# The feed-forward norm of a second-block layer: rows split without the norm's root, the root applied to the results

## What is computed

```python
def rmsnorm(x, g):
    y = x * lax.rsqrt(jnp.mean(x * x, axis=-1, keepdims=True) + EPS)
    return y * g

for l in range(2):
    ...                                                   # three mixers, gated: y
    x = x + jnp.einsum('bsd,de->bse', y, w_out[l])        # output projection
    h = rmsnorm(x, norm_ffn_g[l])
    gu = jnp.einsum('bsd,df->bsf', h, w_ffn_in[l])        # 1024 -> 2 * 2816
    g_ff, u_ff = gu[..., :2816], gu[..., 2816:]
    g_ff = causal_dwconv(g_ff, ffn_conv_w[l], ffn_conv_b[l])   # 3 taps along the rows
    x = x + jnp.einsum('bsf,fd->bsd', silu(g_ff) * u_ff, w_ffn_out[l])
```

## Time and profile before

| | before |
|---|---|
| median of 3 runs | 2688.33 us (2687.64 to 2689.95) |
| the profiled execution | 2689.85 us, span from first to last instruction 2688.0 us |
| PE busy | 2414.5 us, 90% of the span |
| DVE, ACT, POOL busy | 1057.6, 745.9, 650.7 us (39%, 28%, 24%) |
| mean granted clock of TensorE | 0.934 of full speed |
| chain of work that ended last | PE 78%, DMA 7%, DVE 7%, issue 3%, ACT 3% |
| DMA engines | mean 112 GB/s |

### The profile page before, as it was taken

How to read it: one execution, slowest core, us unless ns; L and a number is a source line. 1 busy time by engine, 2 the same in 40 slices (tenths; PEclk the granted TensorE clock), 3 DMA queues, 4 the chain that set the end, 5 groups by cost and what they waited for, 6 DMA issues and landing times.

```text
span 2688.0 us, 31483 instructions
## 1 busy us (share of the span) xinstructions
PE 2414.5 (90%) x12390; PEld 1679.0 (62%) x12390; DVE 1057.6 (39%) x1863; ACT 745.9 (28%) x1176; POOL 650.7 (24%) x284
## 2 busy tenths in 40 slices
PE   7989688896777769989999999998988999999998
PEld 2334466544222248657876888887755887688886
DVE  2455455522011151565243656202165423466610
ACT  2333212211111113323222333212343222233311
POOL 0000000001000024213443444443320444344443
PEclk9999788876888879989998999999998999899999
DMA  4101700043999833212322333222210322233322
GB/s 187 47 24 39 144 3 2 2 178 138 406 411 408 327 110 110 64 32 71 96 93 70 95 100 97 79 99 81 91 55 23 95 94 94 70 95 95 101 80 85
DMA packets 80458, 301.86 MB, mean 112 GB/s; under 512 B 6944, under 2 KB 7328, under 8 KB 79808
## 3 DMA queue, kind: packets, MB, share of 16 engines
q1 hardware_dynamic: 72864, 277.97, 30.2%
q10 hardware_dynamic: 5152, 13.58, 1.3%
q0 software_dynamic: 2304, 8.39, 0.9%
HBM read 283.86 MB, written 24.97 MB: 115 GB/s over the span
## 4 chain that ended last, share of the span: by engine, by line
PE 78%; DMA 7%; DVE 7%; issue 3%; ACT 3%; POOL 0%; SPq 0%; DVEq 0%; ACTq 0%; another core or an unknown queue 0%; POOLq 0%
PE bank L1738 12%; PE bank L1740 12%; PE bank L1739 12%; DMA arena<-in_stream 5%; PE bank L527 5%; PE bank L1412 3%; PE bank L1876 3%; PE bank L1878 3%; PE bank L1877 3%; DVE arena L386 2%; PE bank L834 2%; PE bank L1725 2%; DVE arena L392 2%; PE bank L1723 2%; PE bank L1724 2%
## 5 line engine op out<-in xcount | busy, mean ns | idle before, releaser
L1483 POOL TENSOR_TENSOR ring_low<-ring,W_high 128x1024 fp32r<-128x1024 f32 x264 | 635.1, 2406 | 1080.5 <-ACT W_high L396 1080.5
L1738 PE MATMUL bank<-H_high,W_high 128*128 128x512 f32 x1408 | 562.8, 400 | 21.9 <-DVE H_low L386 11.3
L1739 PE MATMUL bank<-H_low,W_high 128*128 128x512 f32 x1408 | 554.5, 394 | 0.0
L1740 PE MATMUL bank<-H_high,ring_low 128*128 128x512 f32 x1408 | 554.1, 394 | 0.0
L396 ACT ACTIVATE W_high<-ring 128x1024 fp32r<-128x1024 f32 x264 | 279.7, 1060 | 974.7 <-PE bank L1740 603.9
L1738 PEld LDWEIGHTS bank<-H_high,W_high 128*128 128x128 f32 x1408 | 267.5, 190 | 102.8 <-issue 27.6
L1740 PEld LDWEIGHTS bank<-H_high,ring_low 128*128 128x128 f32 x1408 | 268.1, 190 | 57.1
L1739 PEld LDWEIGHTS bank<-H_low,W_high 128*128 128x128 f32 x1408 | 268.6, 191 | 55.1 <-issue 1.0
L396 ACT ACTIVATE arena<-bank 128x512 f32<-128x512 f32 (+4 forms) x275 | 130.3, 487 | 466.0 <-PE bank L809 120.2
L392 DVE SCALAR_TENSOR_TENSOR arena<-arena,bank 128x512 f32<-128x512 f32 (+2 forms) x116 | 55.5, 482 | 480.2 <-ACT arena L400 262.3
L1467 POOL DMA_INDIRECT sorted_x<-arena x8 | 7.9, 982 | 638.2 <-DVE arena L386 636.1
(11 more groups left out here) (222 smaller groups left out, 2955.0 us busy)
## 6 DMA issues: line engine op xcount, KB each, us to landing
ring<-in_stream SPq DMA_DIRECT2D x289, 512.0 KB, 3.6
arena<-in_stream SPq DMA_DIRECT2D x32, 2048.0 KB, 13.8
arena<-in_stream SPq DMA_DIRECT2D x32, 1024.0 KB, 10.6
sorted_x<-in_zero_row SPq DMA_DIRECT2D x1, 8704.0 KB, 49.0
arena<-sorted_x SPq DMA_DIRECT2D x17, 512.0 KB, 15.9
sorted_y<-arena ACTq DMA_DIRECT2D x16, 512.0 KB, 7.0
X<-in_x SPq DMA_DIRECT2D x1, 2048.0 KB, 9.0
out<-X ACTq DMA_DIRECT2D x8, 256.0 KB, 2.9
```

Source lines behind the costliest of these rows:

```text
L1483: G.tensor_tensor(ring_low[:, slot, :], ring[:, slot, :], W_high[:, s % 2, :].bitcast(F32), ALU.subtract).then_inc(po.tells("w_split"), 1)
L1738: mm(ps[:, :], wh[:, k, :], H_high[:, k, :], start=k == 0, stop=False)
L1739: mm(ps[:, :], wh[:, k, :], H_low[:, k, :], start=False, stop=False)
L1740: i = mm(ps[:, :], wl[:, k, :], H_high[:, k, :], start=False, stop=k == KD - 1)
```

## The change

The feed-forward products now run on `X * g_ffn` without the root. As each `wout` bank lands and DVE has added it to `X`, ACT writes the high part of `X * g` right away (`Identity` with the gains as scale, event `Lhh`) and then the squares, and DVE makes the low part in one instruction (event `Lh`) and adds the squares of the chunk to a running sum in `SQL[:, 0]` (event `Lsum` after the last). The sum over the features is one float32 product instead of eight, and stands in PE's order between `ffg0` and `ffu0`. The root goes to a buffer of its own (`ROOT`). DVE multiplies each `ffg` bank by `ROOT` on its way into `GP`, in place of ACT's copy, and there is one further DVE multiplication by `ROOT` for each `ffu`. The split of the slot of `ffu0` on ACT moves behind the last high part and the last square. The halved gate biases are written over themselves in `p2`, and the arena, a filling of the constants and an unused rest shrink to make room for `ROOT`. The transfers are the same but for 8 columns less of one load at the start.

```diff
@@ -201,9 +201,9 @@
     l += [f"gate{b_}_0" for b_ in range(3)]
     for m_ in range(8):
         l += [f"gate{b_}_{m_ + 1}" for b_ in range(3) if m_ < 7] + [f"br{b_}_{m_}" for b_ in range(3)]
-    l += [f"wout{m_}" for m_ in range(8)] + ["ssq4"]
+    l += [f"wout{m_}" for m_ in range(8)]
     for k in range(KF):
-        l += [f"ffg{k}", f"ffu{k}"]
+        l += [f"ffg{k}"] + (["ssq4"] if k == 0 else []) + [f"ffu{k}"]
     l += [f"fo{m_}" for m_ in range(8)]
     return {"A": a, "M": m, "B": [f"bias{h}" for h in range(DH)] + [f"gt{m_}" for m_ in range(8)], "L": l, "F": f}
 
...
@@ -270,12 +270,13 @@
             pass
         H_low = sb("H_low", [P, KD, T], F32R)
         W_high = sb("W_high", [P, 2, TPS * P], F32R)
-        sb("early_rest", [P, nCE + nA1 + nW1 - KD * T - 2 * TPS * P])
+        assert nCE + nA1 + nW1 == KD * T + 2 * TPS * P
         p1 = early[:, nCE:nCE + nA1]
         w1 = early[:, nCE + nA1:nCE + nA1 + nW1]
         cst = sb("cst", [P, nC])
         p2 = sb("p2", [P, nA2])
         small = sb("small", [P, 64])
+        ROOT = sb("root", [P, T])
         with nc.sbuf_tensor("arena", [P, ARENA], F32) as arena:
             pass
         arena_split = sb("arena_split", [P, ARENA], F32R)
...
@@ -1853,14 +1854,12 @@
                     pe.e.wait_ge(*pe.emptied(f"wout{m}"))
                     i = product(f"wout{m}", wh, wl, range(KD), Y_PARTS, ready="Ly" if m == 0 else None)
                     i.then_inc(pe.fills(f"wout{m}"), 1)
-                pe.e.wait_ge(*pe.emptied("ssq4"))
-                ps = bank_of("ssq4")
-                for c in range(KD):
-                    pe.e.wait_ge(*pe.nth("Lsq", KD + c + 1))
-                    i = mm(ps[:, :], cc("ones"), SQL[:, c, :], start=c == 0, stop=c == KD - 1)
-                i.then_inc(pe.fills("ssq4"), 1)
                 for k in range(KF):
                     chunk(f"ffg{k}", first=k == 0)
+                    if k == 0:
+                        pe.e.wait_ge(*pe.emptied("ssq4"))
+                        pe.e.wait_ge(*pe.nth("Lsum", 1))
+                        mm(bank_of("ssq4")[:, :], cc("ones"), SQL[:, 0, :], start=True, stop=True).then_inc(pe.fills("ssq4"), 1)
                     chunk(f"ffu{k}")
                 for m in range(8):
                     pe.e.wait_ge(*pe.emptied(f"fo{m}"))
...
@@ -1994,31 +1993,28 @@
                             sc.e.wait_ge(*sc.nth("Lbgate", 1))
                         if m >= 2:
                             sc.e.wait_ge(*sc.nth("Ly", m - 1))
-                        act_(TL[:, b + 3 * (m % 2), :], ps[:, :], ACT.Tanh, bias=arena_small("bgh", b * 8 + m), scale=0.5).then_inc(sc.takes(f"gate{b}_{m}"), 1)
+                        act_(TL[:, b + 3 * (m % 2), :], ps[:, :], ACT.Tanh, bias=q2("b_gate", b * 8 + m), scale=0.5).then_inc(sc.takes(f"gate{b}_{m}"), 1)
                     if m:
                         split_high(1)
                 split_high(1)
                 log_exp_tables()
                 for c in range(KD):
-                    split_high(1)
+                    if c < KD - 1:
+                        split_high(1)
                     sc.e.wait_ge(*sc.taken(f"wout{c}"))
+                    act_(H_high[:, c, :], X[:, c, :], ACT.Identity, scale=q2("g_ffn", c)).then_inc(sc.tells("Lhh"), 1)
                     act_(SQL[:, c, :], X[:, c, :], ACT.Square).then_inc(sc.tells("Lsq"), 1)
-                sc.e.wait_ge(*sc.filled("ssq4"))
-                ps = bank_of("ssq4")
-                log_of(sc, TL[:, 0, :], ps[:, :], EPS, 1.0 / D)
-                sc.e.wait_ge(sc.chain, sc.n)
-                inverse_root(TL[:, 0, :]).then_inc(sc.takes("ssq4"), 1)
+                split_high(1)
                 for k in range(KF):
                     split_high(1)
-                    sc.e.wait_ge(*sc.filled(f"ffg{k}"))
-                    ps = bank_of(f"ffg{k}")
                     if k == 0:
-                        sc.e.wait_ge(*sc.nth("Lh", 2 * KD))
-                        sc.e.wait_ge(*sc.nth("Lgpad", 1))
+                        sc.e.wait_ge(*sc.filled("ssq4"))
+                        log_of(sc, ROOT[:, :], bank_of("ssq4")[:, :], EPS, 1.0 / D)
+                        sc.e.wait_ge(sc.chain, sc.n)
+                        inverse_root(ROOT[:, :]).then_inc(sc.takes("ssq4"), 1)
+                    sc.e.wait_ge(*sc.taken(f"ffg{k}"))
                     if k >= 2:
                         sc.e.wait_ge(*sc.taken(f"ffu{k - 2}"))
-                    act_(GP[:, k % 2, 2:514], ps[:, :], ACT.Copy).then_inc(sc.takes(f"ffg{k}"), 1)
-                    sc.e.wait_ge(*sc.taken(f"ffg{k}"))
                     act_(TF[:, k % 2, :], GP[:, k % 2, 2:514], ACT.Identity, bias=q2("fcb", k), scale=q2("fcw", 2 * KF + k)).then_inc(sc.tells("Lfc"), 1)
                     split_high(1)
                     sc.e.wait_ge(*sc.nth("Lconv", k + 1))
...
@@ -2206,12 +2198,24 @@
                     dv.e.wait_ge(*dv.filled(f"wout{m}"))
                     ps = bank_of(f"wout{m}")
                     stt(X[:, m, :], ps[:, :], 0.5, X[:, m, :], ALU.mult, ALU.add).then_inc(dv.takes(f"wout{m}"), 1)
-                dv.e.wait_ge(*dv.taken("wout7"))
-                norm_split(dv, "ssq4", lambda c: q2("g_ffn", c))
+                    dv.e.wait_ge(*dv.nth("Lhh", m + 1))
+                    stt(H_low[:, m, :], X[:, m, :], q2("g_ffn", m), H_high[:, m, :].bitcast(F32), ALU.mult, ALU.subtract).then_inc(dv.tells("Lh"), 1)
+                    dv.e.wait_ge(*dv.nth("Lsq", KD + m + 1))
+                    if m:
+                        sq = tt(SQL[:, 0, :], SQL[:, 0, :], SQL[:, m, :], ALU.add)
+                        if m < KD - 1:
+                            st(sq)
+                        else:
+                            sq.then_inc(dv.tells("Lsum"), 1)
+                dv.e.wait_ge(*dv.taken("ssq4"))
                 V.memset(GP[:, :, 0:2], 0.0).then_inc(dv.tells("Lgpad"), 1)
                 for k in range(KF):
                     c = TF[:, k % 2, :]
                     g = GP[:, k % 2, :]
+                    dv.e.wait_ge(*dv.filled(f"ffg{k}"))
+                    if k == 0:
+                        dv.e.wait_ge(*dv.nth("Lgpad", 1))
+                    tt(g[:, 2:514], bank_of(f"ffg{k}")[:, :], ROOT[:, :], ALU.mult).then_inc(dv.takes(f"ffg{k}"), 1)
                     dv.e.wait_ge(*dv.nth("Lfc", k + 1))
                     st(stt(c, g[:, 1:513], q2("fcw", KF + k), c, ALU.mult, ALU.add))
                     stt(c, g[:, 0:512], q2("fcw", k), c, ALU.mult, ALU.add).then_inc(dv.tells("Lconv"), 1)
...
@@ -2219,6 +2223,7 @@
                     dv.e.wait_ge(*dv.nth("Lconv", k + 1))
                     t = TF[:, 5, :]
                     st(stt(t, TF[:, 2 + k % 2, :], 1.0, c, ALU.add, ALU.mult))
+                    st(tt(t, t, ROOT[:, :], ALU.mult))
                     dv.e.wait_ge(*dv.filled(f"ffu{k}"))
                     ps = bank_of(f"ffu{k}")
                     tt(t, t, ps[:, :], ALU.mult).then_inc(dv.takes(f"ffu{k}"), 1)
```

More of the change, by code:

```diff
@@ L54 @@
 R = 6
-ARENA = 55 * 512 + 40
+ARENA = 55 * 512 + 4
 TPS = 8
@@ L1627, in build @@
         BRANCH_PARTS = parts(chunks(*range(37, 45)), chunks(45, 46, 47, 48, 16, 17, 18, 19))
[L1629 removed]
+        TF0 = 512 * 37 + 1028 + 512 * 10
         TF = ch(TF0, 6)
[L1631 removed]
+        HIDDEN_PARTS = parts(chunks(*range(0, KF)), chunks(*range(26, 37)) + [512 * 37 + 1028 + 512 * i for i in range(10)] + [TF0 + 4 * 512])
         assert TF0 + 6 * 512 <= ARENA
[L1633 removed]
+        GP = arena[:, 512 * 37:512 * 37 + 1028].rearrange("p (n w) -> p n w", n=2)
         dunits = [(h, i) for h in range(DH) for i in range(NT)]
```

11 lines of the change are left out of this document (3 added, 8 removed).

## The result

| | before | changed |
|---|---|---|
| median | 2689.14 us (2687.64 to 2691.68, 4 runs) | 2640.60 us (2638.39 to 2641.12, 4 runs) |
| the profiled execution | 2689.85 us, span 2688.0 us | 2640.59 us, span 2638.8 us |
| PE busy | 2414.5 us | 2372.0 us |
| DVE, ACT, POOL busy | 1057.6, 745.9, 650.7 us | 1110.6, 734.5, 653.7 us |
| mean granted clock | 0.934 | 0.941 |

The ratio of the changed kernel to the one before is 0.9818, 95% interval 0.9803 to 0.9832. Faster was right, the size was not.

What follows compares the result with a forecast made beforehand. PE was taken to bound the kernel, with a stall and low clock at the norm before the feed-forward stretch. The median 2688.33 less 37.0 for two layers gave 2651.3 us, range 2648.5 to 2657.

Steps and rivals of the forecast that it cites:

- The stall: PE from `ssq4` to `ffu0`, at the norm: 24.91 and 24.93 us removed, 6.32 to 6.48 coming back in each layer.
- The sign: What would show it right, including no window at a clock below 1.00 between 1404 and 1830.
- the sum: Both layers' gain: 24.91 + 24.93 - 2 x (5.44 + 0.88) = 37.2 us; 37.0 was taken.
- The chain of `wout7`: Last bank to low part for `ffg0`, 2.6 us: ready about 1446.4, wanted at 1448.3, hidden with 1.9 us to spare.
- the thin cover: Split of `ffu0`, covered by the one `ssq4` product: in time by only 0.2 to 0.4 us.
- rival 1: At `ffu0`'s split or `wout7`'s chain, PE still waits 1 to 4 us a layer: 2653.5 to 2660 us; chance 0.10.
- rival 4: At `ffg0`, PE waits for the last rows as before; at three times the chain 3 us a layer, 2657; chance 0.02.
- The one product for eight: Between `ffg0` and `ffu0`, one `ssq4` product of 0.88 us comes back where eight took 7.03 us.
- The loop: Feed-forward loop, 22 times a layer: two added DVE multiplications by `ROOT`, 0.69 us each when free, cost PE nothing.
- rival 2: DVE's loop becomes the bound if `t` times `ROOT` is held: 11.77 us a k, 2690 us; chance 0.05 with similar losses.
- rival 3: In the loop, the multiplication into `GP` is held too: 13.5 us a k, 2766 us, slower; chance 0.03.
- The rest: Biases halved in place, smaller arena, 8 columns less in one load: same instructions on the same engines, worth nothing.

Runs made afterwards that it cites:

- Experiment 4: Changed kernel with the one sum product placed ahead of `ffg0` instead of between `ffg0` and `ffu0`: 2645.15 us, ratio 0.9836.
- experiment 8: Changed kernel without DVE's running sum, with eight products of the squares again between `ffg0` and `ffu0`: 2651.73 us, ratio 0.9861.
- experiment 1: Kernel before with only the new layout: smaller arena, unread `ROOT`, biases halved in place; arena at 116672: 2679.52 us, ratio 0.9966.
- experiment 2: Changed kernel with `p2` and `small` sharing 8 columns, so the arena starts 32 bytes earlier, at 116640: 2645.59 us, ratio 0.9836.
- experiment 11: Changed kernel with the arena right behind the constants and the padded banks `GP` moved to its end: 2632.91 us, ratio 0.9809.
- experiment 6: Changed kernel run once more, nothing altered: 2641.10 us, ratio 0.9818.
- experiment 12: Changed kernel with the arena behind the constants and `GP` at its end, timed again in five rounds: 2638.66 us, ratio 0.9818.

## Where the prediction was right, and where it failed

Forecast were 2651.3 us and a range of 2648.5 to 2657; measured were 2640.6. The mechanism of the main term came out as described, and a term that was put at nothing did not.

- **The stall**: right. 24.91 and 24.93 us became 6.33, nothing new waits there, and the windows from 1400 to 1800 all have a clock of 1.00. The sign had named 1404 to 1830, which was too wide: from 1800 to 1830, where the next layer starts, it is 0.89 (before, from 1826 to 1855, 0.82). By the marks the stretch gave 38.2 us, of which 0.5 is the pace of `fo0`: 37.7 against 37.2 in the sum.
- **The chain of `wout7` and the thin cover** (rivals 1 and 4): right, with 0.67 us to spare. Experiment 4 shows what a wait of 3 us there would have cost: 4.7 us, more than its own length, as the clock falls with it.
- **The one product for eight**: right, 6.0 us a layer by experiment 8.
- **The loop** (rivals 2 and 3): right. Both new instructions ran free and PE never waited. `t` times `ROOT` stands behind the held addition, when POOL is idle, as forecast. The room is one further instruction, not two. One reading for it was weaker than it was said to be: in the earlier trace rows the third bank operation starts at 1398.33, ahead of POOL's 1398.65, so that row doesn't show one that begins beside a split and is not held. The changed kernel does (0.68 at 1512.62 beside POOL's 1512.50).
- **The step that failed** is one sentence: "*The rest* (biases halved in place, smaller arena, 8 columns less in one load): the same instructions on the same engines, nothing." The instructions were the same, but the smaller arena and `ROOT` shifted the buffer from which 1824 matmuls read, and each got some 4.2 ns faster (229.4 for 233.5): 7.6 us where the sum has nothing. Experiments 1, 2 and 11 show that the start byte does it. With it the sum would have been 44.6, and 2643.7 us, still 3 above what was measured. The rows shown before held the hint: a chunk of `wout` took 5.60 us and one of the loop 5.44, the same 24 matmuls of the same shape. I used the two as the two ends of a price and did not ask why they differ.
- **What is left**: 48.8 us in the marks, less 37.7 for the stall and about 7.5 for the pace, is 3.6. Some 2.4 of it stand ahead of the first mark, where two executions of the changed kernel differ by 3.7 (experiment 6), and 1.2 in the mixers of the second layer, where two executions of one kernel differ by 6.8 (experiments 11 and 12). Both are within what one kernel does from one execution to the next, and stall and pace together, 45.3 us, lie just inside the interval of the ratio, 45.2 to 53.0 us. No further cause is needed, and none is excluded.
- **The range** had no room for a side effect. It was built from the ends of the terms in the sum, and the term that failed had been given no ends.

## What to carry to other kernels

A norm's root that commutes with a product can leave the path; what that is worth is decided by the place of the sum in PE's order (4.7 us a layer here) and by the room on the string of the loop that takes the root over, not by an engine's busy share. When an edit changes the size or order of buffers, the matmuls that read them are part of the change: compare the step from one matmul to the next for each moving buffer, before and after. And where two products of one shape run at different paces in the profile, find the reason first; here the kernel before with one unused tensor of 40 columns was 0.6% faster, of which the pace explains 9.1 us, somewhat more than half.
